# Twenty of 24 modulation blocks summed on VectorE instead of multiplied on TensorE, in a two-block transformer kernel on one core

## What is computed

```
m = jax.nn.silu(cond) @ w_ada[i] + b_ada[i]        # w_ada: (2, 1024, 6144)
sh1, sc1, g1, sh2, sc2, g2 = jnp.split(m, 6)
h = rmsnorm(x, g) * (1 + sc1) + sh1
x = x + g1 * mixer(h)                              # layer 0: gated linear attention (GLA); layer 1: latent attention
x = x + g2 * conv_ffn(modulate(x, ..., sh2, sc2))  # two halves of width 2816, 3-tap convolution, silu
```

## Time and profile before

| | |
|---|---|
| Median of 3 runs | 4471.8 us (4471.47 to 4480.17) |
| The profiled execution, its own time | 4470.62 us |
| Its span, first to last instruction | 4468.8 us |
| TensorE, VectorE, ScalarE busy | 92%, 43%, 30% of the span |
| Mean granted TensorE clock | 0.959 of full speed |
| GLA stage with its first projections | from 91 to about 578 us of the span |
| First FFN, `a0` | from 678 to about 1310 us of the span |

### The profile page before, as it was taken

The page is one execution under the profiler, slowest core; times in us unless marked ns, Lnnn a source line. Parts: engine busy times, 40 slices in busy tenths (PEclk is TensorE's granted clock), DMA queues, the critical chain, the costliest instruction groups (busy, mean ns, idle before and its releaser), DMA issues.

```text
span 4468.8 us, 47784 instructions
## 1 busy us (share of the span) xinstructions
PE 4132.4 (92%) x19512; PEld 3049.7 (68%) x19512; DVE 1902.3 (43%) x2995; ACT 1360.8 (30%) x2239; POOL 16.9 (0%) x33
## 2 busy tenths in 40 slices
PE   6999899999978989999878999999988889998999
PEld 3777557888865556887756666578866666656887
DVE  1333115544442225565475532344436754224334
ACT  2222214222234334333133342332222334323222
POOL 0000000000000000000000000000000000000000
PEclk8899999999989999999899999999989999999999
DMA  4231013323220012333211112233232110222331
GB/s 151 67 97 64 29 38 99 109 88 106 90 81 16 26 36 71 95 99 95 65 50 48 52 62 85 58 102 95 85 93 66 50 48 29 85 85 78 97 95 62
DMA packets 381015, 329.32 MB, mean 74 GB/s; under 512 B 12352, under 2 KB 347712, under 8 KB 380672
## 3 DMA queue, kind: packets, MB, share of 16 engines
q1 hardware_dynamic: 378224, 314.89, 23.3%
q0 software_dynamic: 2576, 11.37, 0.8%
HBM read 324.14 MB, written 2.10 MB: 73 GB/s over the span
## 4 chain that ended last, share of the span: by engine, by line
PE 72%; DVE 8%; ACT 5%; issue 2%; DMA 0%; ACTq 0%; DVEq 0%
PE ps L399 53%; PE ps L410 3%; PE ps L412 3%; PE ps L411 3%; PE ps L518 1%; DVE WL L361 1%; ACT WH L353 1%; PE ps L1947 1%; ACT arena_m L1613 1%; PE ps L1573 1%; PE ps L1925 1%; DVE arena_m L1595 1%; DVE arena_m L1590 1%; PE ps L424 1%; PE ps L581 1%
## 5 line engine op out<-in xcount | busy, mean ns | idle before, releaser
L361 DVE TENSOR_TENSOR WL<-ring,WH 128x2048 fp32r<-128x2048 f32 (+3 forms) x221 | 461.3, 2088 | 358.6 <-ACT WH L353 358.3
L353 ACT CAST WH<-ring 128x2048 fp32r<-128x2048 f32 (+3 forms) x221 | 384.1, 1738 | 478.4 <-PE ps L399 386.5
L399 PE MATMUL ps<-MH,WH 128*128 128x512 f32 x1024 | 399.2, 390 | 3.2 <-DVE WL L361 3.2
L399 PE MATMUL ps<-MH,WL 128*128 128x512 f32 x1024 | 398.9, 390 | 0.0
L399 PE MATMUL ps<-ML,WH 128*128 128x512 f32 x1024 | 398.9, 390 | 0.0
L410 PE MATMUL ps<-MH,WH 128*128 128x512 f32 x768 | 342.4, 446 | 13.1 <-DVE WL L361 13.1
L399 PE MATMUL ps<-IH,WH 128*128 128x512 f32 (+1 forms) x880 | 336.4, 382 | 0.0
L399 PE MATMUL ps<-IL,WH 128*128 128x512 f32 (+1 forms) x880 | 326.0, 370 | 0.0
L399 PE MATMUL ps<-IH,WL 128*128 128x512 f32 (+1 forms) x880 | 325.1, 369 | 0.0
L412 PE MATMUL ps<-MH,WL 128*128 128x512 f32 x768 | 309.6, 403 | 0.0
L411 PE MATMUL ps<-ML,WH 128*128 128x512 f32 x768 | 308.9, 402 | 0.0
(11 more groups left out here) (289 smaller groups left out, 6723.8 us busy)
## 6 DMA issues: line engine op xcount, KB each, us to landing
ring<-in_w_in SPq DMA_DIRECT2D x62, 1024.0 KB, 5.2
ring<-in_w_ada SPq DMA_DIRECT2D x48, 1024.0 KB, 8.5
ring<-in_ffn_w_up SPq DMA_DIRECT2D x88, 512.0 KB, 5.2
ring<-in_w_gu SPq DMA_DIRECT2D x88, 512.0 KB, 5.1
ring<-in_ffn_w_down SPq DMA_DIRECT2D x28, 768.0 KB, 4.4
ring<-in_w_down SPq DMA_DIRECT2D x28, 768.0 KB, 4.3
ring<-in_gla_w_in SPq DMA_DIRECT2D x8, 1024.0 KB, 9.6
ring<-in_w_out SPq DMA_DIRECT2D x8, 1024.0 KB, 7.7
```

What stands on the lines that cost most here:

```text
L353: nc.scalar.copy(split_slot(key, WH), raw_slot(key)).then_inc(act_done, mark("act", ("rounded", k)))
L361: nc.vector.tensor_tensor(split_slot(key, WL), raw_slot(key), split_slot(key, WH).bitcast(F32), ALU.subtract).then_inc(dve_done, mark("dve ...
L399: m = nc.tensor.matmul(out, l, r, start=(i == 0), stop=(i == len(pairs) - 1))
```

## The change

Twelve blocks of layer 1 and eight of layer 0 are no longer multiplied on TensorE. A ring piece of such a block is now 512 rows x 512 columns (1 MB as before). VectorE multiplies each 128 x 512 slice with the condition's value of that partition and adds it to a running sum in `spare`: 8 slices x 2 conditions, 16 instructions a block, in four parts q of four instructions. TensorE then sums over the partitions by 8 matmuls with one moving column of ones; the stationary side is the sum, 128 x 128. ScalarE's copy and the turn are gone; VectorE's bias addition stays. The ring slot of the first piece is free when part 1 is done, that of the second when part 3 is done.

In the GLA stage the parts are put between VectorE's fill: of a head's eight, part 0 in step 0, 1 in step 1, 2 and 3 in step 2, 4 and 5 in step 4 and 6 and 7 after the outputs of step 5. TensorE's sums stand in step 3 and at the end of step 5. In the FFN a block goes with each of the up tiles 0, 1, 3, 4, 6, 7, 9, 10, 12, 13, 15 and 16: its two pieces follow the piece of that tile, parts 0 and 1 stand between the convolution and the multiplication (L1275), parts 2 and 3 after the subtraction (L1229), and TensorE sums it after the next up tile.

```diff
+        ADA1 = [0, 1, 3, 4, 6, 7, 9, 10, 12, 13, 15, 16]
+            def ada_rows_of(l, c):
+                for i in range(2):
+                    piece((("ada", l, c), i), [(0, cols(io["w_ada"][l][512 * i:512 * i + 512, :], 512 * c, 512 * c + 512))])
-                ada(0, 4 + 2 * h)
-                ada(0, 5 + 2 * h)
+                ada_rows_of(0, 4 + 2 * h)
+                ada_rows_of(0, 5 + 2 * h)
-                        if j % 2:
-                            extra(j // 2)
+                        extra(j)
-            def ada1(c):
-                ada(1, c)
-                if c == FT // 2 - 1:
-                    ada(1, c + 1)
+            def ada1(j):
+                if j in ADA1:
+                    ada_rows_of(1, ADA1.index(j))
...
+        def ada_part_dve(l, c, q):
+            if q == 0:
...
+                    nc.vector.wait_ge(pe_done, at(("ada_turned", l, c - 1)))
+            key = (("ada", l, c), q // 2)
+            n, loads_n = where[key]
+            if q % 2 == 0:
+                nc.vector.wait_ge(slot_loaded[n % SLOTS], loads_n)
+            w = raw_slot(key).rearrange("p (t n) -> p t n", n=512)
+            for k in range(2 * q, 2 * q + 2):
+                for s in range(2):
+                    acc = ada_sums[:, s, :]
+                    x = w[:, k % 4, :]
+                    if k == 0:
+                        m = nc.vector.tensor_scalar(acc, x, cond[:, k, s:s + 1], None, ALU.mult)
+                    else:
+                        nc.vector.wait_ge(dve_done, at(("ada_part", l, c, k - 1, s)))
+                        m = nc.vector.scalar_tensor_tensor(acc, x, cond[:, k, s:s + 1], acc, ALU.mult, ALU.add)
+                    m.then_inc(dve_done, mark("dve", ("ada_part", l, c, k, s), *([used(key)] if k % 4 == 3 else []),
+                                              *([("ada_sum", l, c)] if k == DT - 1 else [])))
+        def ada_sum_pe(l, c, bank=None):
+            nc.tensor.wait_ge(dve_done, at(("ada_sum", l, c)))
+            out = take(("ada_turned", l, c), bank)
+            for j in range(4):
+                for s in range(2):
+                    m = nc.tensor.matmul(out[:, 2 * j + s:2 * j + s + 1], ada_sums[:, s, 128 * j:128 * j + 128], ones[:, :],
+                                         start=True, stop=True)
+            m.then_inc(pe_done, mark("pe", ("ada_turned", l, c)))
...
-                   [("v", 2), ("v", 3), ("ada", 0)], [("v", 4), ("v", 5), ("ada", 1)], [("kt", 0), ("kt", 1), ("turn", 0)]]
+                   [("v", 2), ("v", 3), ("ada", 0)], [("v", 4), ("v", 5)], [("kt", 0), ("kt", 1), ("ada", 1)]]
...
-        PROJ_DVE = [[("min", 0), ("min", 1), ("B", 0)], [("B", 1), ("QD", 0)], [("QD", 1), ("KI", 0)],
-                    [("KI", 1), ("KS", 0)], [("KS", 1)], [("ada", 0), ("ada", 1)]]
+        PROJ_DVE = [[("min", 0), ("min", 1), ("B", 0), ("sum", 0)], [("B", 1), ("QD", 0), ("sum", 1)],
+                    [("QD", 1), ("KI", 0), ("sum", 2), ("sum", 3)],
+                    [("KI", 1), ("KS", 0)], [("KS", 1), ("ada", 0), ("sum", 4), ("sum", 5)], [("sum", 6), ("sum", 7), ("ada", 1)]]
...
@@ def conv_dve
+                extra(j, 0)
                 nc.vector.wait_ge(act_done, at(("silu", tag, j)))
...
                 rest_inter_dve(tag, j, t0)
-                if j % 2:
-                    extra(j // 2)
+                extra(j, 1)
...
+        def ada1_pe(j):
+            if j - 1 in ADA1:
+                ada_sum_pe(1, ADA1.index(j - 1))
+        def ada1_dve(j, i):
+            if i == 0 and j - 1 in ADA1:
+                ada_dve(1, ADA1.index(j - 1))
+            if j in ADA1:
+                for q in (2 * i, 2 * i + 1):
+                    ada_part_dve(1, ADA1.index(j), q)
...
-                if i >= SLOTS and plan[i - SLOTS][2]:
+                if i >= SLOTS and (plan[i - SLOTS][2] or plan[i - SLOTS][0] in summed_pieces):
                     sp.wait_ge(dve_done, at(("slot_used", i - SLOTS)))
```

More of the change, by code:

```diff
@@ L125, in build @@
         sel = sb("sel", [P, 2])
+        ones = sb("ones", [P, 1])
         modv = sb("modv", [P, 2, 48, 2])
@@ L304, in build @@
         weights_list()
+        summed_pieces = [(("ada", l, c), i) for l, c0 in ((0, 4), (1, 0)) for c in range(c0, 12) for i in range(2)]
         where = {}
@@ L504, in square_act @@
                 nc.scalar.wait_ge(pe_done, at(("hsq_read", key, i - 2)))
-            elif ("ada_turned", 1, 10 + i) in counts.at and key == "n1":
-                nc.scalar.wait_ge(pe_done, at(("ada_turned", 1, 10 + i)))
+            elif key == "n1":
+                nc.scalar.wait_ge(pe_done, at(("ada_turned", 1, 11)))
             nc.scalar.activation(NSQ[:, i % 2, 0:tn], X[:, n, t0:t0 + tn], ACT.Square).then_inc(
@@ L626, in ada_act @@
                 act_done, mark("act", ("ada_rows", l, c), ("free", ("ada", l, c))))
+        ada_sums = spare
+        def ada_part_dve(l, c, q):
+            if q == 0:
+                if (l, c) == (1, 0):
+                    for t0 in (0, CTX):
+                        nc.vector.wait_ge(pe_done, at(("hms", "n0f", t0)))
+                elif (l, c) == (0, 4):
+                    nc.vector.wait_ge(pe_done, at(("ada_turned", 0, 3)))
+                else:
[11 more added lines that the diff above has]
+                        m = nc.vector.tensor_scalar(acc, x, cond[:, k, s:s + 1], None, ALU.mult)
+                    else:
+                        nc.vector.wait_ge(dve_done, at(("ada_part", l, c, k - 1, s)))
[10 more added lines that the diff above has]
+            m.then_inc(pe_done, mark("pe", ("ada_turned", l, c)))
         def ada_dve(l, c):
@@ L733, in start_dve @@
             nc.vector.memset(eps[:, :], EPS).then_inc(dve_done, mark("dve", ("eps",)))
+            nc.vector.memset(ones[:, :], 1.0).then_inc(dve_done, mark("dve", ("ones",)))
             nc.vector.memset(cond[:, :, :], 0.0).then_inc(dve_done, mark("dve", ("cond0",)))
@@ L834, in proj_pe @@
             elif what == "ada":
[L835 to L838, removed]
+                ada_sum_pe(0, 4 + 2 * h + i, spare_bank())
             else:
@@ L895, in proj_act @@
                     act_done, mark("act", ("V", h), ("free", ("v", h, i))))
-            elif what == "ada":
-                ada_act(0, 4 + 2 * h + i)
             else:
@@ L903, in proj_act @@
                                        act_done, mark("act", ("KT", h, i), ("free", ("kt", h, i, half))))
-        PROJ_DVE = [[("min", 0), ("min", 1), ("B", 0)], [("B", 1), ("QD", 0)], [("QD", 1), ("KI", 0)],
-                    [("KI", 1), ("KS", 0)], [("KS", 1)], [("ada", 0), ("ada", 1)]]
+        PROJ_DVE = [[("min", 0), ("min", 1), ("B", 0), ("sum", 0)], [("B", 1), ("QD", 0), ("sum", 1)],
+                    [("QD", 1), ("KI", 0), ("sum", 2), ("sum", 3)],
+                    [("KI", 1), ("KS", 0)], [("KS", 1), ("ada", 0), ("sum", 4), ("sum", 5)], [("sum", 6), ("sum", 7), ("ada", 1)]]
         def proj_dve(h, what, i):
             p = h % 2
-            E = gb["E", i] if what != "ada" else None
+            E = gb["E", i] if what not in ("ada", "sum") else None
             if what == "min":
@@ L942, in proj_dve @@
                 nc.vector.tensor_tensor(E, gb["K"], E, ALU.mult).then_inc(dve_done, mark("dve", ("KS", h, i)))
+            elif what == "sum":
+                ada_part_dve(0, 4 + 2 * h + i // 4, i % 4)
             else:
@@ L2645, in subln_gain_dve, with nothing @@
             nc.vector.wait_ge(dve_done, at(("sg", l)))
[L2648 to L2669, removed]
+        def ada1_pe(j):
[7 more added lines that the diff above has]
+                    ada_part_dve(1, ADA1.index(j), q)
+        def nothing(*_):
             pass
@@ L2742, in _ @@
             hnorm_act(hnorms["n0f"])
-            conv_ffn_act("a0", 0, ALL, ada1_act, hnorms["n1"])
+            conv_ffn_act("a0", 0, ALL, nothing, hnorms["n1"])
             ln_exp_tables()
```

6 lines of the change are left out of this document (2 added, 4 removed).

## The result

| | before | after |
|---|---|---|
| Median | 4471.64 us (4 runs, 4469.06 to 4480.17) | 4540.53 us (4 runs, 4538.98 to 4548.23) |
| Span of the profiled execution | 4468.8 us | 4540.0 us |
| Mean granted TensorE clock | 0.959 | 0.949 |

What follows compares the result with a forecast made beforehand. TensorE, busy 92% of the span, was taken to bound the kernel, with VectorE's free half between fixed times. GLA +24 and FFN +39 gave +63 us on 4470.6, 4534; with the median 1.2 higher, 4535 us, range 4488 to 4580.

Steps and rivals of the forecast that it cites:

- the GLA term: GLA stage: late sums at the heads' ends and in the first projections, plus half-clock sums, cost +24 us.
- the FFN term: FFN: group 0, the later groups, group 6 and the end together cost +39 us.
- A block on TensorE gains 1.0 us: TensorE, each block: 2.8 us removed, 16 instructions of 1.8 us added; 20 us in all at best.
- Sums at 0.67 us: VectorE: each scalar_tensor_tensor of 128x512 takes 0.67 us; a block takes 10.2 us.
- rival (a): VectorE's sums take 0.8 us each, slower than a free run; about 4562 us; chance 0.22, including more such waits.
- The slot holds up tile 3g+2: FFN: the ring slot is freed only after part 3, at E+15.6 (E ends tile 3g), so TensorE idles 7 us.
- rival (b): FFN: transfers land early enough and VectorE alone limits; a group takes about 81 us, the kernel 4480; chance 0.14.
- A group of 90 us: FFN groups 1 to 5: 90 us each against 79.6, +51 us in all.
- the 1.6 us by which VectorE was to hold up the down product: FFN, each group: VectorE's queued work delays the first addition, so the seventh result waits 1.6 us for its bank.
- Group 0 +13, group 6 -3, the end -22: FFN: group 0 loses 13 us, group 6 drops one block (-2.8), waits after the last up tile go (-22).
- The second wait of a head's end: GLA heads' ends: TensorE waits about 6 us for VectorE before the sum's matmuls.
- Rival (c): Whole kernel: VectorE's sums hidden everywhere, TensorE gains 1.0 us in 18 blocks plus 22 at the end; 4432 us; chance 0.09.

Runs made afterwards that it cites:

- `ring`: The changed kernel with an FFN block's two modulation pieces one up tile later in the ring list: 4502.65 us, ratio 1.0069 to before.
- `place`: The kernel before, all blocks on TensorE, with the FFN's twelve moved to the up tiles used by the change: 4450.35 us, ratio 0.9956.
- `warm`: The changed kernel plus 3 and 7 dummy TensorE matmuls at the two waits in step 5 of heads 0 to 2: 4524.83 us, ratio 1.0120 to before.
- `both`: The changed kernel with FFN modulation pieces later in the ring and GLA parts and first ring pieces moved earlier: 4434.15 us, ratio 0.9916 to before.
- `order_place`: The kernel before with state updates first in GLA steps 3 and 4 and FFN blocks moved, no sums on VectorE: 4439.00 us, ratio 0.9927.
- `order_only`: The kernel before with VectorE's state updates ahead of the fill in GLA steps 3 and 4: 4460.83 us, ratio 0.9974.

## Why the prediction was right, point by point

**Right in sign, size and mechanism.** 4540.5 was measured where 4535 was said. That the figure is within 6 us is in part luck, for its parts are further off, with opposite signs: the GLA term was 16.7 us too small, the FFN term 8.5 too large.

- *A block on TensorE gains 1.0 us.* Right: 16 instructions take 1.84 us (1.8 forecast) at full clock. In the GLA stage six of the eight sums ran at half clock, 3.52 to 3.58, and there a block costs more than the 2.8 us of before.
- *Sums at 0.67 us, rival (a) at 0.8.* Right: eight take 5.38 to 5.39 us, 0.67 each. Rival (a) falls. The first two, tensor_scalar, take 0.44 each (0.43 forecast).
- *The slot holds up tile 3g+2, rival (b) that VectorE alone does.* Shown by `ring`: with the slot's place mended, the group falls to 80.6 us, which is rival (b)'s 81. Release, landing, split and idle time of the group shown came within 0.3 us of the forecast (over the six groups the wait was 6.84 to 8.66 us).
- *A group of 90 us.* Four of the five take 88.4, the first 90.0 (443.6 in all, 450 forecast). The term that is missing is the 1.6 us by which VectorE was to hold up the down product: TensorE's waits for L1364 from 790 to 1235 us are 0.2 us in all, and it is VectorE that waits for TensorE's results there, 24.0 us in 30 waits. Four times 1.6 is 6.4 of the 6.8 us by which the groups were forecast too long, and most of the 8.5 of the FFN term.
- *Group 0 +13, group 6 -3, the end -22.* They were +12.1, -3.0 and -22.8 (of which the end of the FFN by itself is -24.6, and +1.8 came behind it); that the gain at the end is due to placement was shown by `place`. The end of after shows no wait, one unbroken piece of the chain:

```profile
1214.94 97.08 PE ps L404 x561
```

- *GLA: +24.* The mis-sized term; it measured 40.7. The second wait of a head's end was right (6.14 in all three heads). The first was right in head 0 (3.34) and fell to 2.52 and 0.91 in heads 1 and 2. The half clock is what was too small: it was charged only to the sum behind the second wait, three times 1.6 us. Set beside the same matmuls of before, it costs more at these places:
  - the sum in the first projections, 3.57 where I had 1.9 (1.7 of the 2.4 us missed there);
  - the starts of heads 0, 2 and 3, which take 1.9, 1.7 and 2.1 us longer than in before;
  - the outputs of head 0, 3.52 instead of 1.90;
  - step 3 of head 0, which became 1.5 us longer where I had counted 1.3 as gained, step 3 of head 2 (1.5) and the norm's matmuls in step 4 of head 2 (3.60 instead of 1.98);
  - the 16 matmuls behind the first 5.2 us wait of head 3, a wait that before has too, 10.05 instead of 8.67.

  Together that is about 16 us, of which head 1 has none; for heads 1 and 2 the forecast was an estimate for the whole head, so these places cannot be set against it one by one. The start of head 1 is not among them: its 13.6 us at 0.50 are no loss, since before runs there at half clock too. The list is read from the traces. `warm` shows by a run that filling the waits brings the clock back at the heads' ends and behind them (1.00 from 240 to 275 us). For step 3, which has only the wait of 1.85 us that before has too, the cause of the longer half clock stays open.
- *Rival (c), hidden everywhere, 4432.* It fell for the kernel as written. Its point of decision in the FFN, the list order, was the right one. That `both` gives nearly its figure, 4434, is a coincidence: rival (c) had 18 us from TensorE's shorter blocks, and in `both` all but some 5 us come from the places of the FFN's blocks and the order of the state updates (`order_place`).

A further miss: that the order of before held some 12 us of its own (`order_only`) was there to be read in the earlier trace rows, where the state updates start only behind the operation that waited 8.8 us.

## What to carry to other kernels

Moving work to an engine that is idle on average also moves the moment at which it frees buffers: before moving it, follow every slot that the new user releases to the piece that waits for it in the fixed list, and shift the list by one where it is late (one word gave 38 of 69 us here). Charge a new wait of some us on TensorE not with its length alone but with the half clock of the matmuls that follow (behind the six waits of 6.84 to 8.66 us in the FFN of after it was 0.50 to 0.61 over the next 4.8 us), and look first which of those run at half clock already. Split a change into its engine part and its placement part and time each: here most of the gain to be had was placement and order. And when a fix gives back about the time that was missed, lay it beside the kernel before place by place, to see that it is the same time.

## What the runs showed of the hardware

- TensorE's clock fell to 0.50 in step 3 of head 0 although the engine had idled for only 1.9 us just before. This is the window ahead of the fall (clock 1.00, TensorE busy 1.15 of 3.0 us); the next, from 223 us on, is shown above with 0.50. Before has the same idle time there and falls too, to 0.58 for 3.1 us (the second window):

```profile
220.00:223.00 3.00, 1.15 (x10) 1.01 (x10) 2.96 (x6) 0.47 (x1) 0.00 (x0) 1.00 0.00 0
```

```profile
216.20:219.30 3.10, 3.10 (x33) 1.34 (x32) 1.27 (x3) 0.00 (x0) 0.00 (x0) 0.58 0.02 5
```

- The clock was at 0.50 while the trace shows no idle time of TensorE: at the start of head 1 in before it was busy in all of these 9 us. The whole stretch of 62 instructions took 22.53 us there and 14.30 in `warm`, which differs from after only by the fillers:

```profile
246.00:255.00 9.00, 9.00 (x33) 6.66 (x32) 6.64 (x13) 2.74 (x4) 0.00 (x0) 0.50 0.01 4
```

- Matmuls with one moving column pay the half clock in full: 16 instructions took 1.84 to 1.95 us at full clock and 3.52 to 3.58 at half. In the window from 223 us on the weight loads are busy 4.93 of 5.00 us.
- Adding 30 useless matmuls of 512 columns (60 instructions, 6.23 us for the 7 of one head's end) made the kernel 15.7 us faster.
